# Scaling the matrix-memory heads' weights on ScalarE in place of VectorE, in a two-block transformer kernel on one core

## What is computed

```python
b = jnp.cumsum(lf, axis=-1)
dmat = jnp.where(tri, b[..., :, None] - b[..., None, :] + li[..., None, :], -jnp.inf)
m_t = jnp.maximum(m_inter, jnp.max(dmat, axis=-1))
p = jnp.exp(dmat - m_t[..., None]) * jnp.einsum('bhtd,bhsd->bhts', qb, kb)
num = ... + jnp.einsum('bhts,bhsv->bhtv', p, vb)
den = ... + jnp.sum(p, axis=-1)
h = num / jnp.maximum(jnp.abs(den), jnp.exp(-m_t))[..., None]
```

## Time and profile before

| | us |
|---|---|
| median of 3 runs | 2670.47 |
| lowest, highest run | 2667.81, 2671.71 |
| the profiled execution | 2667.92 |
| its span, first to last instruction | 2666.1 |
| TensorE busy in it | 2564.8 |
| VectorE busy | 1957.1 |
| ScalarE busy | 1614.5 |

### The profile page before, as it was taken

The page is one execution under the profiler, slowest core; times in us unless marked ns, Lnnn a source line. Parts: engine busy times, 40 slices in busy tenths (PEclk is TensorE's granted clock), DMA queues, the critical chain, the costliest instruction groups (busy, mean ns, idle before and its releaser), DMA issues.

```text
span 2666.1 us, 65659 instructions
## 1 busy us (share of the span) xinstructions
PE 2564.8 (96%) x27832; PEld 2159.6 (81%) x27832; DVE 1957.1 (73%) x1886; ACT 1614.5 (61%) x1688; POOL 378.9 (14%) x440
## 2 busy tenths in 40 slices
PE   9999999999999999999999999999999999999998
PEld 8887788888887888898788888789777687786775
DVE  5467575565567765666775566798999999999997
ACT  4345664353356654455654445657888787888876
POOL 3214022122115222103022103031000000000000
PEclk9999999999999999999999999998999999999999
DMA  8574365555554555654465665478999999999996
GB/s 270 169 208 131 104 198 197 168 188 189 163 152 152 192 176 178 197 166 141 138 200 200 174 197 166 123 261 338 410 420 422 418 411 422 415 419 418 411 421 274
DMA packets 354985, 666.18 MB, mean 250 GB/s; under 512 B 24545, under 2 KB 285825, under 8 KB 315825
## 3 DMA queue, kind: packets, MB, share of 16 engines
q1 hardware_dynamic: 353920, 661.39, 68.9%
q0 software_dynamic: 528, 0.63, 0.3%
q10 hardware_dynamic: 288, 0.59, 0.1%
HBM read 661.49 MB, written 1.05 MB: 249 GB/s over the span
## 4 chain that ended last, share of the span: by engine, by line
PE 60%; DVE 20%; DMA 7%; ACT 6%; issue 4%; DVEq 2%; POOLq 0%; ACTq 0%; SPq 0%; POOL 0%
PE ps L2331 17%; PE ps L2333 17%; PE ps L2332 17%; DVE w_lo L1619 7%; DMA w<-in_moe_units 3%; DVE w_lo L1459 3%; DVE work L1619 2%; DVE ff L1619 2%; DMA mix<-in_moe_units 2%; ACT w_hi L955 2%; ACT w_hi L846 2%; DMA squares_and_low<-in_moe_units 1%; PE ps L2374 1%; PE ps L2380 1%; PE ps L2375 1%
## 5 line engine op out<-in xcount | busy, mean ns | idle before, releaser
L2331 PE MATMUL ps<-x_hi,w_hi 128*128 128x96 f16 (+2 forms) x5024 | 1077.0, 246 | 26.5 <-DVE w_lo L1619 6.6
L2333 PE MATMUL ps<-x_hi,w_lo 128*128 128x96 f16 (+2 forms) x5024 | 1076.3, 246 | 5.2 <-issue 5.1
L2332 PE MATMUL ps<-squares_and_low,w_hi 128*128 128x96 f16 (+2 forms) x5024 | 1076.4, 246 | 5.0 <-issue 4.9
L1459 DVE SCALAR_TENSOR_TENSOR w_lo<-w,w_hi 128x2048 f16<-128x2048 f32 (+3 forms) x335 | 693.9, 2082 | 295.1 <-ACT w_hi L846 293.4
L846 ACT ACTIVATE w_hi<-w 128x2048 f16<-128x2048 f32 (+3 forms) x335 | 556.8, 1671 | 85.6 <-PE ps L2333 74.8
L2331 PEld LDWEIGHTS ps<-x_hi,w_hi 128*128 128x128 f16 x5024 | 493.1, 98 | 82.8 <-issue 22.0
L2332 PEld LDWEIGHTS ps<-squares_and_low,w_hi 128*128 128x128 f16 x5024 | 492.8, 98 | 51.8 <-issue 7.0
L2333 PEld LDWEIGHTS ps<-x_hi,w_lo 128*128 128x128 f16 x5024 | 492.8, 98 | 48.4 <-issue 6.2
L2332 PE MATMUL ps<-ff,w_hi 128*128 128x272 f16 (+1 forms) x880 | 243.3, 276 | 0.0
L2333 PE MATMUL ps<-ff,w_lo 128*128 128x272 f16 (+1 forms) x880 | 243.3, 276 | 0.0
L2331 PE MATMUL ps<-ff,w_hi 128*128 128x272 f16 (+1 forms) x880 | 243.3, 276 | 0.0
(11 more groups left out here) (408 smaller groups left out, 4772.7 us busy)
## 6 DMA issues: line engine op xcount, KB each, us to landing
w<-in_ffn_w_up_units SPq DMA_DIRECT2D x176, 512.0 KB, 4.6
w<-in_moe_units SPq DMA_DIRECT2D x75, 1024.0 KB, 12.0
w<-in_moe_units SPq DMA_DIRECT2D x56, 1280.0 KB, 15.5
w<-in_w_in SPq DMA_DIRECT2D x112, 512.0 KB, 4.7
mix<-in_moe_units SPq DMA_DIRECT2D x50, 1024.0 KB, 12.0
mix<-in_moe_units SPq DMA_DIRECT2D x36, 1280.0 KB, 15.7
w<-in_mix_w_in SPq DMA_DIRECT2D x60, 512.0 KB, 4.9
squares_and_low<-in_moe_units SPq DMA_DIRECT2D x26, 1024.0 KB, 11.9
```

The costliest lines, as they stand in the source:

```text
L1459: vec.scalar_tensor_tensor(k.w_lo[:, s, 0:size], k.w32[:, s, 0:size], WS, k.w_hi[:, s, 0:size], ALU.mult, ALU.subtract).then_inc(k.parts_r ...
L2331: pe.matmul(acc, w_hi, x_hi, start=first, stop=False)
L2332: pe.matmul(acc, w_hi, x_lo, start=False, stop=False)
L2333: return pe.matmul(acc, w_lo, x_hi, start=False, stop=last)
```

## The change

VectorE's last instruction for an ml item, the multiply of the rows by the reciprocal, and the drain before it are removed. The reciprocal gives a new semaphore, `ml_inverted`. ScalarE has a new instruction per ml item, a Copy with the reciprocal as its per-row scale, in the place where fox items have theirs: in step n + 1 for item n, behind the exponentials of item n + 1. It gives `ml_probs_ready`, on which the transposes wait as before.

```diff
+    k.ml_inverted = sem("ml_inverted")
...
+        def ml_scale(b, keys):
+            pr = k.pr2[:, b, 0:keys]
+            act.activation(pr, pr, ACT.Copy, scale=k.stat[:, b, 6:7]).then_inc(k.ml_probs_ready, 1)
+
...
             if kind == "fox":
                 act.wait_ge(k.sum_inverted, fox0 + of_kind(n)[0] + 1)
                 softmax_norm(n % BUFS, P, P * (j + 1), pr=k.pr2)
+            else:
+                act.wait_ge(k.ml_inverted, ml0 + of_kind(n)[1] + 1)
+                ml_scale(n % BUFS, P * (j + 1))
...
-            vec.reciprocal(k.stat[:, b, 6:7], k.stat[:, b, 5:6])
-            vec.drain()
-            vec.tensor_scalar(pr, pr, k.stat[:, b, 6:7], None, ALU.mult).then_inc(k.ml_probs_ready, 1)
+            vec.reciprocal(k.stat[:, b, 6:7], k.stat[:, b, 5:6]).then_inc(k.ml_inverted, 1)
```

## The result

| | before | after |
|---|---|---|
| median, us | 2667.83 | 2674.09 |
| lowest, highest of 15 runs | 2665.83, 2671.71 | 2669.14, 2678.66 |
| the profiled execution | 2667.92 | 2675.63 |
| its span | 2666.1 | 2673.5 |

The ratio of after to before is 1.0022, 95% interval 1.0015 to 1.0030: the changed kernel is slower by 5.9 us (4 to 8; the two medians differ by 6.3). The median of before came down by 2.6 us as more runs were added. The forecast was +2.7 us. That its time of 2673.1 lies only 1.0 us beside the measured one is luck: that time was counted from the three first runs. So there are two things to explain: where the 2.7 is, and where 3 more come from.

The account below looks back on a forecast made before the run. TensorE, busy 96% of the span, was taken as the bound, losing time where it waits, lastly for ScalarE's group copy. Delays of 1.28 and 1.39 us gave +2.7 on 2670.5, so 2673.1 us, range 2668.2 to 2678.0.

Parts of the forecast that it names:

- ScalarE's wait for the reciprocal: In ScalarE's queue after item 9's exponentials: 0.42 us waiting plus 0.29 of scaling, 0.71 ahead of copies and high split.
- each new scaling stands some 0.4 us behind the exponentials: Sign that the forecast is right, on ScalarE: every added scaling starts about 0.4 us after the exponentials ahead of it.
- The low splits of units 7 and 8 wait for ScalarE: Sign on VectorE: these weight splits wait for ScalarE's high splits, starting 0.32 and 0.17 us later in the first layer.
- The wait before item 12: TensorE's second wait, for the weighing of item 10: 0.92 us grows by 0.32 to about 1.2 in the first layer.
- The walked sum: Delay of TensorE's start on gated unit 8, followed through the queues: 1.28 us first layer, 1.39 second, +2.7 together.
- the last wait: TensorE's 0.79 us wait before gated unit 8, for ScalarE's group copy to empty its bank; said to decide among four.
- Relief as a rival: VectorE alone sets the path: item 13's multiply gone, later steps 0.43 us earlier per layer; -0.9 us, 2669.6, chance 0.16.
- The delays add up: Rival: late ScalarE delays low splits, masks and exponentials in turn, 2.95 us a layer; +5.9 us, 2676.4, chance 0.12.
- a distance that grows by 3: Sign of accumulating delays: item 10's score to unit 8's first product, 25.70 us in the first layer, lengthens by 3.
- Does it reach the end?: Step after both layers: TensorE's next wait, 1.23 us at 1300.54, moves along and absorbs nothing, so +2.7 us reaches the end.

Follow-up runs that it names:

- late-scaling kernel: Changed kernel with ScalarE's matrix-memory scaling moved to the end of its step, behind copies and high split; 2667.67 us, ratio 0.9997 to the kernel before.
- filled kernels: Small unread matmuls added in TensorE's waits ahead of item 16's score and unit 8: changed kernel 2671.19 us (1.0013), kernel before 2666.62 us (0.9995).
- the changed kernel's second profile: The changed kernel run once more with nothing altered, beside the kernel before on the same chip; 2674.26 us, ratio 1.0020.
- items 14 and 15 kept: The change for items 8 to 13 only, VectorE scaling items 14 and 15 as in the kernel before; 2669.39 us, ratio 1.0006 to that kernel.

## Why the forecast was right, and where it was short

- **ScalarE's wait for the reciprocal.** Right. Predicted 0.42 us idle and 0.29 of work ahead of the copy. Measured 0.33 idle and 0.31 of work at items 8, 10, 12 and 14; the 0.09 is the tail of the exponentials, which the forecast had counted as idle. The sign "each new scaling stands some 0.4 us behind the exponentials" was too wide, also by the forecast's own walk: of the wide ones 9, 13 and 15 don't wait, and 11 waits 0.57.
- **The low splits of units 7 and 8 wait for ScalarE.** Right: 1.12 and 0.20 us.
- **The wait before item 12.** Predicted 1.2, measured 1.25 in both layers.
- **The walked sum.** Predicted 1.28 and 1.39, measured 1.32 and 1.45. The steps between are right as well: the score of item 12 came 0.32 later, as predicted, that of item 16 0.19 later against 0.17. The late-scaling kernel shows that the place in the queue is the price, and the kernel in which only items 14 and 15 moved shows that most of it is paid at the end of the ml items. What the forecast didn't see is that the last wait only hides the earlier delays: with the group copy moved ahead and that wait gone, 0.37 of the 1.33 us remain.
- **Relief as a rival.** The mechanism is real and was undersized: one multiply off the path counted, two are (0.85 in place of 0.43). It lost all the same, as ScalarE's part is worth 2.17.
- **The delays add up.** Its +5.9 us is the measured number, by another cause. Its own sign, a distance that grows by 3, isn't there: it grew by 1.3 and 1.5. A total that fits proves no mechanism.
- **Does it reach the end?** Here a step fell short. I let both layers' delays through and asked only for a later wait that might take them up. I had no term for TensorE's granted clock. The earlier trace rows gives 1.00 for the stretch before the change, and I took it for given while I lengthened a wait from 0.79 to 1.74 some 5 us behind another long one. The measured difference is 5.9 us against a term of 2.67. Of the missing 3.1, falls of the clock behind that wait make 2.2 on average by their count, 1.1 by the times of the filled kernels. The 1.6 us of the first profile's fall aren't among them: it began ahead of the lengthened wait, and such falls came without the change too.
- **What stays open.** 1 to 2 us of the mean, and 3.0 of the 7.4 us in the first profile. Of these 3.0, 2.5 come behind unit 12 of layer 1. In the changed kernel's second profile nothing comes there: it reaches that unit at 1729.56, 6.0 us behind the kernel before, and its span of 2672.1 is 6.0 longer. But for some tenths, all of the difference lies in the two stages. In the twelve profiles other than before's and the changed kernel's first, this last part takes from 1.2 us less to 1.7 more than in before's. The first profile had the lower clock in it, for instance here, where the kernel before has 1.00:

```profile
2440.00:2480.00 40.00, 37.15 (x566) 30.08 (x564) 35.87 (x14) 30.85 (x15) 0.00 (x0) 0.91 1.01 422
```

The kernel before has such stretches too, at other times (0.97 from 2560 to 2600, where the changed kernel has 1.00). Over its 15 runs the mean clock is 0.9901 in the changed kernel; in before it is 0.9918 to 0.9922, over 33 runs on each of three chips. Whether a later stream of expert weights brings some of those falls about, or each execution has its own, no run here settles; the second profile speaks for the latter. The intervals (2 us on either side) would also allow no remainder at all.

The Trainium skill, "ScalarE: Activation LUTs", section "Rules for kernel authors", gives plain multiplies to VectorE. The changed kernel agrees in direction (1.0022). The late-scaling kernel doesn't: with the same multiplies on ScalarE it is no slower than before (0.9997).

## What to carry to other kernels

Before an instruction goes to the less busy engine, ask what stands behind it in that engine's queue and whether its operand is there when its turn comes: some 0.3 us of idle and 0.3 to 0.4 of work an item ahead of the splits and the group copy cost 1.3 us a layer, and with the same instructions at the end of the step the kernel was no slower than before. Order by who is waited for, what releases a bank or a buffer first and what nobody waits for last. Where an edit lengthens a wait of TensorE behind another long one, put the granted clock into the sum as a chance with a price, from the matmuls' durations at either level. And before a fall is put down to a wait, look which of the two came first.

## What the runs showed of the hardware

TensorE's granted clock fell from 1.00 to 0.50 in stages in which TensorE was nowhere idle for longer than 1.74 us at a time: three times behind a single wait of 1.57 or 1.71 us, four times behind two waits, of 1.57 or 1.72 and of 1.74 us, some 5 us apart with matmuls between. It stayed at 0.50 for 3.4 us in five of the seven cases and for 6.8 in two. A fall cost 1.6 to 1.7 us, and 2.4 in the one case in which TensorE had no wait in 6.8 us of it (layer 0 with items 14 and 15 kept). It came and went from one execution and one layer to the next: the same changed kernel had it in one layer in one profile and in both in the other, at different places. With two to five small matmuls in the waits, whose results nobody reads, it did not fall (0 of 6 stages against 7 of 22, which is too few to be sure), and they cost no time that the distances show.
